# Loading MoE expert weights in 4 MB units and computing a block's gates and up-projections token-major

## The chip, the core and the metric

One NeuronCore of a Trainium2 chip runs the whole kernel. The metric is the device time of one execution in microseconds (us), lower is better. Engines: PE is TensorE (matmuls; PEld is its weight load), DVE is VectorE, ACT is ScalarE, POOL is GpSimd, and SP is the sequencer that issues most DMAs.

## The reference

One decoder layer on 256 tokens of width 1024, in float32. Cut to what matters here:

```python
proj = rmsnorm(x) @ w_in                      # 1024 x 5632
q_a, k_a, v_a, q_b, f_b, i_b, g_b, gate_a, gate_b = split(proj)
mixed = sigmoid(gate_a) * (y_a @ moba_up) + sigmoid(gate_b) * (y_b @ hgrn_up)
x = x + mixed @ w_out
h2 = rmsnorm(x);  top 4 of 32 experts for every token
gu = h2 @ w_gate_up[e] + b_gate_up[e]         # 1024 x 2048 = 8 MB for each expert
act = (clip(gu[1::2]) + 1) * swiglu(gu[0::2])
x = x + weight * (act @ w_down[e] + b_down[e])   # 1024 x 1024 = 4 MB for each expert
```

All 32 experts' weights are read, 12 MB each (the MB of this text are units of 1024 KB), 384 MB in all.

## The kernel before

**Front.** Projections run as split products: each weight piece is rounded to a high part on ACT (`round_hi`) and the rest is formed on DVE (`form_lo`, line 388), and PE adds high x high, low x high and high x low. `split_T` (line 1325) makes a 256-feature piece feature-major: the weights are the stationary side, 256 tokens move, 48 matmuls of 256 columns for a piece (24 where the depth is 512). `split` (line 1342) makes a unit token-major: 128 tokens are the stationary side and 512 weight columns move, 24 matmuls of 512 columns. The eight gate pieces ga0..3 and gb0..3, and the up-projections mu0..3 and hu0..3, use `split_T`; their mix is therefore feature-major as the output projection `mixed()` (line 1496) needs it. The list `PIECES` (line 47) sets the order and the buffer of every rounded piece, and `bank_units()` (line 66) the order of PE's units and who drains each.

**Expert weights.** There are 11 slots of 2 MB (16 KB in each partition): eight in S, then M's last four pages, EXTRA and B. A pair of experts takes 12 loads of 2 MB: 0 to 3 and 4 to 7 are gate/up weights, 8 to 11 the down weights. They go round the ring (`ring`, line 377), each by one DMA of 16 KB runs on SP's queue (`load`, line 403). SP issues a load once PE has used what was in its slot (`used`, line 447; `load_pair`, line 456). PE waits on a semaphore of each slot (`arrived`, line 1656). The last pair's last two loads go in parts of 8 KB and 4 KB runs, so that little is left when the last byte lands (line 475).

The pair-0 loads are issued early, between the loads of the front, as their space comes free (lines 408 to 445): 9 after the 10th weight group, 0 before the load of `mu`, 1 before `wo0`, 10 and 3 before `wo1`, 5 after hu3, 8 after the mix, 2 and 6 after the first half of the output projection and 4 and 7 after the second.

**Expert pair.** PE's loop `pair` (line 1753): `gate_up` (line 1664) for both experts of the pair, with weight columns in blocks of 512 as the moving side; `down` (line 1717); `gather` (line 1626), which reads the token rows X with a step of two elements (`hidden`, line 1586) as the stationary side; and `combine` (line 1648). The gate/up biases come in by four DMAs of 128 KB on ACT's queue (line 725), are rounded in one ACT copy (line 752) and one DVE subtract (line 1207), before ACT can do the router's exponentials (line 755).

Of the kernel before, what the change touches and what calls it, by code (L numbers as in the profile page):

```python
# [11 lines left out]
P = 128  # L12
T = 256
TT = T // P
D = 1024
# [26 lines left out]

GATES = [("g0", GB, 0), ("g1", GB, 1)] + [(f"ga{j}", GA0 + j // 2, j % 2) for j in range(4)] + \
# [10 lines left out]
    [("wo0", j, "dve", ("C", j), None) for j in range(2)] + \  # L54
    [("wo1", j, "dve", ("A", j), f"hu{2 * j + 1}") for j in range(2)]
# [10 lines left out]
def bank_units():  # L66
# [9 lines left out]
    for h in range(0, HEADS, 2):  # L76
# [5 lines left out]
    u += [(f"mu{j}", "dve") for j in range(4)] + [(f"hu{j}", "dve") for j in range(4)]  # L82
# [9 lines left out]
            "pos0": 5, "pos1": 2, "all": 7, "wT": 6}  # L92
UNITS = bank_units()
# [29 lines left out]
def hybrid_block(nc, A, out):  # L123
    ctx = ExitStack()
    with ctx:
# [7 lines left out]
        with ExitStack() as early:  # L133
# [3 lines left out]
            hT_hi = over("hT_hi", 2).rearrange("p (k t) -> p k t", k=KD)  # L137
            over("skip_b2", 1, F32)
            FRONT = early.enter_context(nc.sbuf_tensor("FRONT", [P, 512], F32))[:]
            MSK = early.enter_context(nc.sbuf_tensor("MSK", [P, 512], I32))[:, 0:NMASK * CHUNK]  # L140
            MSK = MSK.rearrange("p (m t) -> p m t", t=CHUNK)
# [9 lines left out]
            over("skip_s0", 8, F32)  # L151
# [3 lines left out]
            w_lo = [over(f"w_lo{s}", 4) for s in range(RING)]  # L155

        with ExitStack() as later:
            later.enter_context(nc.sbuf_tensor("skip_m0", [P, 1024 * 9], F32))  # L160
# [7 lines left out]
        B = sb("B", [P, 4096])  # L168
        XN = B[:, 0:TT * D].rearrange("p (t d) -> p t d", t=TT)
        M = sb("M", [P, 12 * 1024])  # L170


        S = sb("S", [P, 8, 4096])
# [14 lines left out]
        SF = S[:].rearrange("p s n -> p (s n)")  # L188
# [21 lines left out]
        def mpage(n, c=1):  # L210
            return M[:, 1024 * n:1024 * (n + c)]
# [5 lines left out]
        mixT = mpage(2, 2).rearrange("p (k t) -> p k t", k=KD)  # L217
# [4 lines left out]
        gaT, gbT = mpage(8, 2), mpage(10, 2)  # L222
# [5 lines left out]
        bias_raw = mpage(6)  # L228
        DN_B = mpage(6)[0:E, :]
        FW = mpage(6)  # L230
# [15 lines left out]
        EXTRA = sb("EXTRA", [P, 4096])  # L246
        slots = [S[:, s, :] for s in range(8)] + [mpage(8, 4), EXTRA[:], B[:]]

# [26 lines left out]
        def hi_part(where):  # L275

            buf, j = where
            if buf == "Q":
                return hi_a[:, 1024 * j:1024 * j + 1024].rearrange("p (k n) -> p k n", k=4)
            return {"A": hi_a, "B": hi_b, "C": hi_c}[buf][:, 2048 * j:2048 * j + 2048].rearrange("p (k n) -> p k n", k=KD)  # L280

# [12 lines left out]
        def bank(name):  # L294
            return PS[BANK_OF[AT_UNIT[name]]]


# [20 lines left out]
        osq_ready, rms_ready, sig_ready, yb_ready, mix_ready = (  # L318
            sem(n) for n in ("osq_ready", "rms_ready", "sig_ready", "yb_ready", "mix_ready"))
# [10 lines left out]
        mix_hi_ready, mix_lo_ready = sem("mix_hi_ready"), sem("mix_lo_ready")  # L330
# [4 lines left out]
        slot_loaded = [sem(f"slot_loaded{s}") for s in range(SLOTS)]  # L335
# [33 lines left out]
        wgu = A["w_gate_up"].rearrange("l e (s p k) n -> (l e) s p (k n)", p=P, k=2)  # L369
        wdn = A["w_down"].rearrange("l e (h p c) n -> (l e) h p (c n)", p=P, c=4)  # L370
        gu_slot = [w.rearrange("p (k n) -> p k n", k=2) for w in slots]
        dn_slot = [w.rearrange("p (k n) -> p k n", k=4) for w in slots]
# [4 lines left out]
        def ring(j, m):  # L377

            return (12 * j + m) % SLOTS, (12 * j + m) // SLOTS

        PER_ROUND = [(6 * E - 1 - n) // SLOTS + 1 for n in range(SLOTS)]

        def slot_src(e, m):

            src = wgu[e + m // 4, m % 4] if m < 8 else wdn[e + (m - 8) // 2, m % 2]
            return src[0] if len(src.shape) == 3 else src
# [12 lines left out]
        def _(sp):  # L399
# [3 lines left out]
            def load(e, j, m):  # L403

                slot = ring(j, m)[0]
                sp.dma_start(slots[slot], slot_src(e, m)).then_inc(slot_loaded[slot], 16)

            for n, what in enumerate(LOADS):
                if what == GB1:
                    load(0, 0, 9)  # L410
                if what == "mu":
                    filled(sp, "kT1")
                    load(0, 0, 0)
# [3 lines left out]
                if what == "wo1":  # L417
                    load(0, 0, 10)
# [37 lines left out]
            def load_pair(p, e, j, stop=12):  # L456
# [6 lines left out]
            for part, done in ((0, half_loaded), (1, slot_loaded[0])):  # L463
# [1404 lines left out]
```

## Time and profile before

| what | value |
|---|---|
| median of 3 runs | 1136.11 us (1135.65 to 1136.47) |
| the profiled execution, its own time | 1136.25 us |
| its span in the trace | 1134.5 us |
| PE busy | 1059.2 us (93%) |
| DVE / ACT / POOL busy | 348.4 / 222.7 / 38.9 us |
| moved by DMA | 439.17 MB (here 10^6 bytes), mean 387 GB/s |
| share of SP's queue in the 16 DMA engines' time | 92.6% |
| TensorE clock granted | full in all 40 slices |

The profile is one execution. "Busy" adds up an engine's instructions; the DMA share is the mean busy share of the 16 DMA engines, and packets of one engine overlap a little, so it can read 1.01. The front (everything ahead of the experts) ends near 221 us, the experts near 1124 us.

### The profile page before, as it was taken

How to read it: one execution, taken by the hardware profiler on the slowest of the kernel's cores; microseconds unless marked ns; L12 is line 12 of the kernel's file. 1: busy time of each engine (PE TensorE's matmuls, PEld its weight loads, DVE VectorE, ACT ScalarE, POOL GpSimd, SP SyncE). 2: the span in 40 equal slices, each digit the busy share in tenths (PEclk: the TensorE clock that was granted, in tenths of full speed). 3: DMA queues.
4: the chain of work that ended last, by engine and by line, in shares of the span. 5: the costliest groups of instructions: out<-in, count | busy, mean ns of one | idle time of the engine just before them, and what ended most of it. 6: DMA issues, size and time to landing. Idle time of an engine off the chain costs nothing.

```text
span 1134.5 us, 13360 instructions
## 1 busy us (share of the span) xinstructions
PE 1059.2 (93%) x5613; PEld 519.9 (46%) x5613; DVE 348.4 (31%) x686; ACT 222.7 (20%) x354; POOL 38.9 (3%) x32
## 2 busy tenths in 40 slices
PE   7999999999999999999988888888888898899896
PEld 7889999734343443434333333333333334233332
DVE  4984788422303222222222222222112020303022
ACT  6645674201010101011010010101010101010002
POOL 0390000000000000000000000000000000000000
PEclk9999999999999999999999999999999999999999
DMA  9545669999999999999999999999999999999994
GB/s 320 190 150 215 231 215 365 368 415 415 430 428 428 426 430 427 428 428 427 429 426 428 427 428 428 428 429 426 429 428 428 428 426 428 428 427 427 428 425 201
DMA packets 47489, 439.17 MB, mean 387 GB/s; under 512 B 5388, under 2 KB 7848, under 8 KB 22600
## 3 DMA queue, kind: packets, MB, share of 16 engines
q1 hardware_dynamic: 45136, 436.71, 92.6%
q10 hardware_dynamic: 2296, 1.61, 0.5%
q8 instruction: 47, 0.77, 0.3%
q14 instruction: 10, 0.08, 0.0%
HBM read 437.26 MB, written 1.05 MB: 386 GB/s over the span
## 4 chain that ended last, share of the span: by engine, by line
PE 57%; DMA 41%; DVE 1%; issue 0%; ACT 0%; another core or an unknown queue 0%; DVEq 0%
DMA S<-in_w_gate_up_dram 21%; PE PS L1671 20%; DMA S<-in_w_down_dram 12%; PE PS L1730 9%; PE PS L1338 9%; DMA B<-in_w_gate_up_dram 4%; PE PS L1652 4%; DMA EXTRA<-in_w_gate_up_dram 4%; PE PS L1632 3%; PE PS L1351 1%; PE PS L1354 1%; PE PS L1357 1%; PE PS L1712 1%; PE PS L1692 1%; PE PS L1318 1%; PE PS L1389 1%
## 5 line engine op out<-in xcount | busy, mean ns | idle before, releaser
L1671 PE MATMUL PS<-S,M 128*64 128x512 f32 x1520 | 340.0, 596 | 28.5 <-DMA S<-in_w_gate_up_dram 22.0
L1671 PEld LDWEIGHTS PS<-S,M 128*64 128x64 f32 x1520 | 105.3, 137 | 241.9 <-issue 195.7
L1171 DVE TENSOR_SCALAR M<-PS 128x256 f32<-128x256 f32 x64 | 27.0, 423 | 531.8 <-PE PS L1671 531.8
L1730 PE MATMUL PS<-S,M 128*64 128x512 f32 x736 | 164.7, 595 | 17.1 <-DMA S<-in_w_down_dram 17.1
L765 ACT ACTIVATE M<-M 128x256 f32<-128x256 f32 x64 | 26.7, 417 | 495.4 <-DVE M L1171 495.4
L1730 PEld LDWEIGHTS PS<-S,M 128*64 128x64 f32 x736 | 52.0, 137 | 119.8 <-issue 102.5
L770 ACT COPY M<-PS 64x512 f32<-64x512 f32 x31 | 17.9, 578 | 276.4 <-PE PS L1730 276.4
L1185 DVE COPY M<-PS 128x512 f32<-128x512 f32 x32 | 22.1, 692 | 127.7 <-PE PS L1712 127.7
L1632 PE MATMUL PS<-M,X 128*128 128x128 f32 x480 | 59.0, 281 | 0.0
L1632 PEld LDWEIGHTS PS<-M,X 128*128 128x128 f32 x480 | 57.7, 196 | 0.0
L1652 PE MATMUL PS<-M,SELT 128*128 128x512 f32 x120 | 55.5, 605 | 0.0
L392 DVE TENSOR_TENSOR w_lo<-S,hi_a 128x2048 fp32r<-128x2048 f32 (+1 forms) x24 | 46.5, 1954 | 20.0 <-ACT hi_a L569 20.0
L1671 PE MATMUL PS<-M 128*64 128x512 f32 x192 | 43.7, 597 | 3.4 <-DMA M<-in_w_gate_up_dram 2.4
L1671 PE MATMUL PS<-EXTRA,M 128*64 128x512 f32 x176 | 39.9, 595 | 3.6 <-DMA EXTRA<-in_w_gate_up_dram 3.6
L1179 DVE TENSOR_TENSOR M<-M 128x256 f32<-128x256 f32 x64 | 38.9, 607 | 2.2
L569 ACT CAST hi_a<-S 128x2048 fp32r<-128x2048 f32 (+1 forms) x24 | 38.4, 1622 | 5.7 <-PE PS L1338 3.2
L1671 PE MATMUL PS<-B,M 128*64 128x512 f32 x160 | 36.3, 596 | 3.4 <-DMA B<-in_w_gate_up_dram 3.4
L1652 PEld LDWEIGHTS PS<-M,SELT 128*128 128x128 f32 x120 | 21.6, 189 | 33.7 <-issue 33.7
L1162 DVE TENSOR_TENSOR M<-PS,SMALL 128x512 f32<-128x512 f32 x32 | 22.1, 692 | 34.1 <-PE PS L1632 32.8
L1338 PE MATMUL PS<-hT_lo,hi_a 128*128 128x256 f32 x224 | 31.6, 283 | 0.0
L1338 PE MATMUL PS<-hT_hi,w_lo 128*128 128x256 f32 x208 | 29.2, 283 | 0.0
L1338 PEld LDWEIGHTS PS<-hT_lo,hi_a 128*128 128x128 f32 x224 | 29.0, 192 | 0.0
(259 smaller groups left out, 978.3 us busy)
## 6 DMA issues: line engine op xcount, KB each, us to landing
S<-in_w_gate_up_dram SPq DMA_DIRECT2D x95, 2048.0 KB, 47.8
S<-in_w_down_dram SPq DMA_DIRECT2D x43, 2048.0 KB, 47.2
M<-in_w_gate_up_dram SPq DMA_DIRECT2D x12, 2048.0 KB, 46.5
EXTRA<-in_w_gate_up_dram SPq DMA_DIRECT2D x11, 2048.0 KB, 48.7
S<-in_w_in_dram SPq DMA_DIRECT2D x10, 2048.0 KB, 7.9
B<-in_w_gate_up_dram SPq DMA_DIRECT2D x10, 2048.0 KB, 48.5
B<-in_w_down_dram SPq DMA_DIRECT2D x7, 2048.0 KB, 48.2
EXTRA<-in_w_down_dram SPq DMA_DIRECT2D x6, 2048.0 KB, 48.0
```

The lines of the kernel that those rows point to most:

```text
L392: tensor_tensor(raw_part(what, j, lo=True), raw_part(what, j), hi_part(PIECES[n][3]), ALU.subtract).then_inc(lo_ready[PIECES[n][2]], 1)
L569: st.did(nc.scalar.copy(hi_part(PIECES[n][3]), raw_part(what, j)), hi_ready)
L765: nc.scalar.activation(sg[:, c], gate[:, c], ACT.Sigmoid, scale=ALPHA).then_inc(sigm_ready, 1)
L1162: v.tensor_tensor(hTe[:, 4 * part:4 * part + 4, :], src[:].rearrange("p (k s) -> p k s", k=4), n2w[:, 4 * part:4 * part + 4].unsqueeze(2). ...
L1171: v.tensor_scalar(gate[:, c], g2[:, :, 0], LIMIT, None, ALU.min).then_inc(gate_ready, 1)
L1179: v.tensor_tensor(act.rearrange("p (c q) -> p q c", c=4)[:, 64 * half:64 * half + 64, :], up[:, c].rearrange("p (q c) -> p q c", c=4), sg[ ...
L1185: v.tensor_copy(actT[b], (gu[1] if b else multi)[:].rearrange("p (c s) -> p c s", c=4)).then_inc(actT_ready, 1)
L1338: ins = mm(ps[:, T * a:T * a + T], w[:, k, P * a:P * a + P], x[:, k, :], start=(k == 0 and w is w_h and x is hi), stop=(k == kn - 1 and x ...
L1632: ins = mm(dst[:, P * a:P * a + P], hidden(tt, 4 * part + a), sel[:, tt, :], start=(tt == 0), stop=(tt == TT - 1))
L1652: mm(acc[tt][n][:], selT[:, P * tt:P * tt + P], Y[:, 512 * n:512 * n + 512], start=False, stop=True, skip_group_check=True)
L1671: ins = mm(gu[half][64 * g:64 * g + 64, :], hTe[:, k, tok], gu_slot[slot][:, kk, c:c + 512], start=(k == 0), stop=(k == KD - 1))
L1730: ins = mm(dst[64 * n:64 * n + 64, :], actT[b][:, k, 64 * kh:64 * kh + 64], dn_slot[slot][:, k, 512 * n:512 * n + 512], start=(kh == 0 and ...
```

## The change

1. A pair's loads are now joined two and two (0+1, 2+3, ... 10+11): one DMA of 4 MB with 32 KB runs into two neighbouring slots, issued when both slots are free. All slots lie in one tensor W so that neighbours adjoin. A unit stays two 2 MB loads (16 KB runs) where its slots are the last and the first of W, in pair 0, in the first four loads of pair 1, and from load 4 on in the last pair (`by_slots`).
2. So that a 4 MB unit is contiguous, a partition holds four rows of the gate/up matrix (before: two) and eight of the down matrix. The gathered rows of X are read with a step of four elements, and the moving weight columns of `gate_up` in blocks of 8 elements with a step of 16.
3. PE waits on semaphores of a pair's load number instead of the slot's.
4. Gates and up-projections are token-major (`split`), and the mixed output is turned by 16 transposes in four units mT0..3, the first three after hu1, hu2 and hu3, and the last inside `mixed()`. ACT rounds and DVE subtracts each turned chunk out of PSUM.
5. A second buffer hi_d, over slot 0, takes the high parts of GA1, GB1 and hu. So load 0 of pair 0 moves from before `mu` to after hu3. In the DVE's order both halves of GA1 come ahead of the softmax; a gate's first unit needs both halves of its group.
6. All biases come twice as wide: eight DMAs of 128 KB (four of them after the last `squares`), four ACT copies and four DVE subtracts of 64 partitions.

```diff
-    [(what, j, "dve", ("A", j % 2), "va1" if n < 2 else GATES[n - 2][0]) for n, (_, what, j) in enumerate(GATES)] + \
-    [("mu", j, "dve", ("Q", j), f"gb{2 + j // 2}") for j in range(4)] + \
-    [("hu", j, "dve", ("Q", j), f"mu{j}") for j in range(4)] + \
+    [(GB, j, "dve", ("A", j), "va1") for j in range(2)] + [(GA0, j, "dve", ("A", j), f"g{j}") for j in range(2)] + \
+    [(GA1, j, "dve", ("D", j), "kT1") for j in range(2)] + [(GB0, j, "dve", ("A", j), "ga1") for j in range(2)] + \
+    [(GB1, j, "dve", ("D", j), "ga3") for j in range(2)] + \
+    [("mu", j, "dve", ("QA", j), "gb1") for j in range(4)] + [("hu", j, "dve", ("QD", j), "gb3") for j in range(4)] + \
...
-        wgu = A["w_gate_up"].rearrange("l e (s p k) n -> (l e) s p (k n)", p=P, k=2)
-        wdn = A["w_down"].rearrange("l e (h p c) n -> (l e) h p (c n)", p=P, c=4)
+        wgu = A["w_gate_up"].rearrange("l e (u p k) n -> (l e) u p (k n)", p=P, k=4)
+        wdn = A["w_down"].rearrange("l e (p c) n -> (l e) p (c n)", p=P)
...
+        def by_slots(j, m, first_round):
+
+            return not first_round or ring(j, m) == 9 or j == 0 or j == 1 and m < 4 or j == PAIRS - 1 and m >= 4
...
+            def load_unit(e, j, m):
+
+                sp.dma_start(slots(ring(j, m), 2), unit_src(e, m)).then_inc(slot_loaded[m], 16)
...
                 if what == GB1:
-                    load(0, 0, 9)
-                if what == "mu":
-                    filled(sp, "kT1")
-                    load(0, 0, 0)
+                    load(0, 0, 8)
...
             filled(sp, "hu3")
+            load(0, 0, 0)
             load(0, 0, 5)
-            sp.wait_ge(mix_ready, 1)
-            load(0, 0, 8)
+            filled(sp, "mT3")
+            load(0, 0, 10)
...
-                for m in range(stop):
-                    used(p + (m - SLOTS) // 12, (m - SLOTS) % 12)
-                    load(e, j, m)
+                for m in range(0, stop, 2):
+                    if by_slots(j, m, first_round):
+                        for n in (m, m + 1):
+                            used(p + (n - SLOTS) // 12, (n - SLOTS) % 12)
+                            load(e, j, n)
+                    else:
+                        for n in (m, m + 1):
+                            used(p + (n - SLOTS) // 12, (n - SLOTS) % 12)
+                        load_unit(e, j, m)
...
             for j in range(4):
-                se.wait_ge(mix_step, j + 1)
-                st.did(nc.scalar.copy(mix_hi[:, 2 * j:2 * j + 2, :], mixT[:, 2 * j:2 * j + 2, :]), mix_hi_ready)
+                filled(se, f"mT{j}")
+                st.did(nc.scalar.copy(mixed_chunk(mix_hi, j), turned_mix(j)), mix_hi_ready)
...
+            def turn_mix(j):
+
+                ps = begin(f"mT{j}")
+                pe.wait_ge(mix_step, j + 1)
+                for a in range(4):
+                    c = unit_cols(j).start + P * a
+                    ins = tr(ps[:, P * a:P * a + P], ga[:, c:c + P], ident)
+                end(ins)
...
-                split_T(f"mu{j}", "mu", j, ya_hi, ya_lo, (ya_lo_ready, 2), kn=4)
+                up("mu", "mu", j, ya_hi, ya_lo, (ya_lo_ready, 2))
             pe.wait_ge(o_hi_ready, 1)
             for j in range(4):
-                split_T(f"hu{j}", "hu", j, o_hi, o_lo, (yb_ready, 1), kn=4)
+                up("hu", "hu", j, o_hi, o_lo, (yb_ready, 1))
+                if j:
+                    turn_mix(j - 1)
...
-                return X[:, tt, 256 * (k // 2) + k % 2:256 * (k // 2) + 256:2]
+                return X[:, tt, 512 * (k // 4) + k % 4:512 * (k // 4) + 512:4]
...
+                    cols = gu_slot[slot][:, kk, 1024 * half:1024 * half + 1024].rearrange("p (j g r) -> p j g r", g=2, r=8)
                     for g in range(2):
-                        c = 1024 * g + 512 * half
-                        ins = mm(gu[half][64 * g:64 * g + 64, :], hTe[:, k, tok], gu_slot[slot][:, kk, c:c + 512],
-                                 start=(k == 0), stop=(k == KD - 1))
+                        ins = mm(gate_rows(half, g), hTe[:, k, tok], cols[:, :, g, :], start=(k == 0), stop=(k == KD - 1))
```

## Rows read from the trace of the kernel before

**Rows 1.** Stretches: busy of PE, PEld, DVE, ACT, POOL; TensorE clock; DMA share; GB/s.

```profile
300.00:500.00 200.00, 200.00 (x955) 78.64 (x952) 43.84 (x111) 21.77 (x38) 0.00 (x0) 1.00 1.01 428
500.00:900.00 400.00, 361.32 (x1689) 138.82 (x1689) 77.74 (x192) 39.05 (x69) 0.00 (x0) 1.00 1.01 428
```

**Rows 2.** Chain that ended last, experts: start us, us, what.

```profile
276.32 10.30 PE PS L1671 x48
...
328.16 10.30 PE PS L1671 x48
...
726.37 3.65 PE PS L1671 x16
...
785.07 3.65 PE PS L1671 x16
...
1075.73 44.03 DMA S<-in_w_down_dram
```

**Rows 3.** Groups by line: count, busy us, mean ns, idle before with releasers.

```profile
L1671 PE MATMUL PS<-S,M 128*64 128x512 f32 x1520 | 340.0, 596 | 28.5 <-DMA S<-in_w_gate_up_dram 22.0 <-issue 4.6 <-DVE M L1173 1.8
...
L1632 PE MATMUL PS<-M,X 128*128 128x128 f32 x480 | 59.0, 281 | 0.0
```

**Rows 4.** Stretches of 2 KB, then 8 KB runs; columns as above.

```profile
181.00:186.00 5.00, 5.00 (x44) 5.00 (x43) 4.96 (x5) 0.62 (x1) 0.00 (x0) 1.00 1.04 387
1107.00:1113.00 6.00, 4.79 (x24) 1.95 (x26) 1.81 (x4) 0.20 (x1) 0.00 (x0) 1.00 1.01 419
```

**Rows 5.** DMA view: packets, MB, share; issues: count, size, median us to landing.

```profile
q1 hardware_dynamic: 45136, 436.71, 92.6%
...
S<-in_moba_up_dram SPq DMA_DIRECT2D x1, 2048.0 KB, 7.8
...
M<-in_b_gate_up_dram ACTq DMA_DIRECT2D x4, 128.0 KB, 10.6
```

**Rows 6.** SP's queue in order of time: start us, us until the last issue.

```profile
118.45 0.58 SPq L406 DMA_DIRECT2D S<-in_w_gate_up_dram  x1
...
186.99 0.33 SPq L406 DMA_DIRECT2D S<-in_w_gate_up_dram  x1
...
197.89 14.96 SPq L406 DMA_DIRECT2D S<-in_w_gate_up_dram  x4
222.74 2.04 SPq L468 DMA_DIRECT2D S<-in_w_down_dram  x2
227.89 29.36 SPq L406 DMA_DIRECT2D S<-in_w_gate_up_dram  x7
...
272.93 0.33 SPq L406 DMA_DIRECT2D B<-in_w_down_dram  x1
```

**Rows 7.** Line 406 between 240 and 245 us: the issue and its landing.

```profile
L406 SPq DMA_DIRECT2D S<-in_w_gate_up_dram x1: 328/328/328, 241.6 to 241.6; - x1
...
DMA to landing us min/median/max: 10.7/10.7/10.7
```

**Rows 8.** Chain, front: split (first two), a gate piece, then gb3 to hu3.

```profile
83.62 2.04 PE PS L1351 x8
85.65 1.81 PE PS L1354 x8
...
141.32 5.75 PE PS L1338 x48
...
157.96 28.99 PE PS L1338 x240
```

**Rows 9.** PE's groups by line, 100 to 222 us.

```profile
L1566 PE MATMUL PS<-CST,X 128*128 128x128 f32 x16 | 2.4, 274 | 0.1
```

**Rows 10.** DVE in order of time around the first scores.

```profile
113.84 2.29 DVE L392 TENSOR_TENSOR w_lo<-S,hi_a 128x2048 fp32r<-128x2048 f32 x1 [7.02 <-ACT hi_a L569]
118.91 0.56 DVE L995 TENSOR_TENSOR M<-PS,FRONT 128x384 f32<-128x384 f32 x1 [2.78 <-PE PS L1409]
```

**Rows 11.** ACT in order of time, same place.

```profile
113.71 1.07 ACT L560 COPY M<-PS 128x512 f32<-128x512 f32 x2
```

More of the change, by code:

```diff
@@ L150, in hybrid_block @@
             hi_b = over("hi_b", 4)
-            over("skip_s0", 8, F32)
+            hi_d = over("hi_d", 4)
+            over("skip_s1", 4, F32)
             hi_c = over("hi_c", 4)
@@ L242, in hybrid_block, with slots @@
         wT = mpage(7)[0:E, 512:768]
-        EXTRA = sb("EXTRA", [P, 4096])
-        slots = [S[:, s, :] for s in range(8)] + [mpage(8, 4), EXTRA[:], B[:]]
+        def slots(n, count=1):
+            at = (n + 1) % SLOTS
+            return W[:, 4096 * at:4096 * (at + count)]
         def h3(ap):
@@ L674, in _ @@
             gate_out(2)
-            round_hi(*GATES[4][1:])
             transposed_out("kT", kT)
+            for j in range(2):
+                round_hi(GA1, j)
             gate_out(3)
             for h in range(0, HEADS, 2):
-                round_hi(*GATES[5 + h // 2][1:])
+                round_hi(GB1 if h >= 4 else GB0, h // 2 % 2)
                 exps(h)
@@ L1009, in softmax_norm @@
                        prob_ready)
-            for n in range(2, 5):
-                lo(*GATES[n][1:])
+            for what in (GA0, GA1):
+                for j in range(2):
+                    lo(what, j)
             for h in range(0, HEADS, 2):
@@ L1338, in split_T, with split @@
                             ins = mm(ps[:, T * a:T * a + T], w[:, k, P * a:P * a + P], x[:, k, :],
-                                     start=(k == 0 and w is w_h and x is hi), stop=(k == kn - 1 and x is lo))
+                                     start=(k == 0 and w is w_h and x is hT_hi), stop=(k == KD - 1 and x is hT_lo))
                 end(ins)
-            def split(name, what, tt, hi=hT_hi, lo=hT_lo, lo_there=(hT_lo_ready, 1)):
+            def split(name, what, tt, hi=hT_hi, lo=hT_lo, lo_there=(hT_lo_ready, 1), kn=KD, half=0):
@@ L1348, in split @@
+                w_l = w_lo[s].rearrange("p (k n) -> p k n", k=kn)[:, :, 512 * half:512 * half + 512]
                 rows = slice(P * tt, P * tt + P)
-                pe.wait_ge(hi_ready, n + 1)
-                for k in range(KD):
-                    mm(ps[:].rearrange("p (j n) -> p j n", j=2), hi[:, k, rows], w_h[:, k], start=(k == 0), stop=False)
-                wait_lo(what, 1)
-                for k in range(KD):
-                    mm(ps[:], hi[:, k, rows], w_l[:, k, :], start=False, stop=False)
+                pe.wait_ge(hi_ready, last + 1)
@@ L1355, in split @@
+                for k in range(kn):
+                    mm(ps[:].rearrange("p (j n) -> p j n", j=2), hi[:, k, rows], w_h[:, k, 2 * half:2 * half + 2],
+                       start=(k == 0), stop=False)
+                wait_lo(what, 2 * half + 1)
+                for k in range(kn):
+                    mm(ps[:], hi[:, k, rows], w_l[:, k], start=False, stop=False)
                 pe.wait_ge(*lo_there)
-                for k in range(KD):
-                    ins = mm(ps[:].rearrange("p (j n) -> p j n", j=2), lo[:, k, rows], w_h[:, k], start=False,
-                             stop=(k == KD - 1))
+                for k in range(kn):
+                    ins = mm(ps[:].rearrange("p (j n) -> p j n", j=2), lo[:, k, rows], w_h[:, k, 2 * half:2 * half + 2],
+                             start=False, stop=(k == kn - 1))
@@ L1476, in _ @@
             probs_T(7)
-            split_T(*GATES[8])
+            split(*GATES[8])
             wait_drained(pe, "pT7")
```

253 lines of the change are left out of this document (141 added, 112 removed).

## The prediction

> **What bounds the kernel now.** I read the long stretches first: from 300 to 900 us the 16 DMA engines are busy all the time (share 1.01) and move 428 GB/s, and this doesn't change whether PE is busy for 200 of 200 us or for 361 of 400 [rows 1]. Then the chain of waits, which says who follows whom. Early on it runs through PE: pairs of experts start 328.16 - 276.32 = 51.8 us apart. Later it runs through DMAs that take 47 us to land, and the same point of a pair comes every 785.07 - 726.37 = 58.7 us [rows 2]. A pair is 24 MB, 25.17 million bytes, and at 428 GB/s that is 58.8 us. So PE needs 52 us for what the DMA engines bring in 59. It first lives on the loads made ahead and then waits, and its slack is 7 us for each pair. The last wait of all is for the last down weights: the chain's last DMA, 1075.73 + 44.03 = 1119.8 us [rows 2], with some 15 us of work behind it. The end is therefore set by three things: how many bytes are left when the DMA engines get busy for good, whether they idle after that, and their rate. What PE, ACT or DVE save or lose counts only where it moves one of the three.
>
> **The rate.** The trace has three run lengths with the engines full. In the stretch where half of w_out comes in (2 KB runs) they move 387 GB/s; in the last loads (8 KB runs) 419 [rows 4]; with 16 KB runs 428 [rows 1]. For one of 16 engines 2 KB then take 84.7 ns and 16 KB 612.5 ns. A line through both has 36.8 ns for each KB of 1000 bytes and 9.3 ns for a packet, whatever its size. It gives 422 GB/s for 8 KB, near the 419 of the row. A run of 32 KB replaces two packets by one and saves the 9.3 ns. A 4 MB unit has eight such runs on each engine: 74 ns less. Units: pairs 1 to 15 have 90 couples of loads; 2 of pair 1 and 4 of the last pair stay single, and 8 straddle the ends of W (ring place 9 on an even load: pairs 1, 3, 5, 7, 9, 10, 12, 14). That leaves 76, and 76 x 74 ns = **5.6 us gained**. Nothing in the trace is longer than 16 KB, so I bound it: 0 if longer runs are cut at 16 KB; and 8.0 us from the two nearest rows alone (8 KB 312.8 ns, so 13.1 ns for a packet). I take 5.6 because it lies on the longer base. The queue's 45136 packets [rows 5] should fall by 76 x 128 = 9700.
>
> **Idle at the start.** Space for load 0 of pair 0 is lost until hu3, since hi_d lies in slot 0. Today that load goes out at 118.45 us [rows 6], when the engines are half idle; now it goes out with load 5, at 186.99 in today's times. That is 2 MB, 4.9 us, more in the crowded stretch. But the stretch has holes. Loads 4 and 7 wait for the end of the output projection (the last of the four issues that begin at 197.89 ends at 212.85), the two half loads go at 222.74, and pair 1's first at 227.89 [rows 6]. A lone 2 MB load lands 7.8 us after its issue [rows 5] and moves for 4.9 us, so 2.9 us are latency. I went through the stretch load by load with these two numbers: before, about 6 us pass idle between load 5 and pair 1's load 9, of which 2 to 3 ahead of 227.89. The moved load fills most of that. The other four bias DMAs add 0.5 MB, 1.2 us.
> A new hole comes with the first 4 MB units. Loads 4 and 5 of pair 1 today go out one by one, in a row of seven issues 29.36 us long, 4.8 us apart [rows 6]. As a unit they wait for the second slot. The load ahead of them lands 10.7 us after its issue at 241.6, at 252.3 [rows 7]; the unit goes out at about 251.6 and its bytes flow from 254.5 on. That is a hole of 3 to 4 us. The next units lose nothing, as 4 MB are then under way, and what the row's gap before the load of 272.93 leaves idle today closes again. My replay ends with pair 1's last load landing 1.0 us later than before. From there the lead only grows (PE gives slots back faster than they fill). Bounds: +5 (hole and biases, nothing absorbed) and -1.
>
> **The front.** PE has no idle time there, so what it does counts. A gate piece takes 5.75 us, a token-major unit 2.04 + 1.81 + 1.81 = 5.66, or 5.46 without the first one's overlap [rows 8]: 8 x 0.2 = 1.6 to 2.3 us off. The eight up-projection units take (28.99 - 5.75)/8 = 2.9 us and will take 2.75: 1.2 off. On top come 16 transposes at 2.4/16 = 0.15 us [rows 9]: 2.4 added. One wait is new: ga2 needs both low parts of GA1, and ACT can round them only behind its two kT copies, from 114.8 on [rows 11]. With two roundings and, behind the first, two DVE subtracts of 2.29 [rows 10], the second low part is there near 121, by my reckoning 1 us after PE wants it. The softmax behind them moves from 118.91 [rows 10] to 121, which PE's order covers: it turns the first probabilities only after all of ga2 and two more scores. The mix steps end before PE comes back from the next up-projection. Net 0 to 1 us off; I take 0.2.
> The biases: four copies and four subtracts of 64 x 512 replace one of each. They must be there before the third step of the first gate/up, 10 us after 221. Landing 10.6 us [rows 5] after an issue near 212.85 (the output projection's end), plus some 4 us of work, is in time by 3 us.
>
> **PE in the pairs.** The moving weights are now read in 32-byte pieces and X with a step of four elements; the numbers of matmuls stay. I price both at nothing. A pair has 128 gate/up matmuls of 340.0/1520 = 0.224 us, 28.6 us, and 32 gather matmuls of 0.123 us, 3.9 us [rows 3]. What hides a slowdown is the 7 us of slack; the gather could take 2.5 times as long, the gate/up a quarter more.
> The Trainium skill, SBUF — State Buffer, section "Door 1: The DMA port swizzle", speaks against the step of four: SBUF has lines of 16 bytes, and a read that has only one hit in each line pays. By that page the gather's operand would slow, the 32-byte pieces would not. No run here shows it; it is a rival below.
>
> **Sum**, against the profiled execution's own 1136.25 us: -5.6 (rate) + 1.0 (start) - 0.2 (front) = 1131.45. The median of the runs lies 0.14 lower, so **1131.3 us**. About 0.2% (2.3 us) is what a measurement of this kernel can tell from no change.
>
> **Rivals.**
> *No gain in rate* (0.18). For: packets may be cut at 16 KB, or 428 GB/s may be the wall of something else than packets. Against: three run lengths lie on one line. Time: 1136.1 + 0.8 = 1136.9.
> *The gather slows* (0.10). A step of four elements doubles the weight reads. In the pairs 3.9 us more still fits into 7. But the first gather stands ahead of the first expert, with 32 matmuls, and puts off the slots that loads from 222.74 on wait for [rows 6]. The hole ahead of 227.89, which the moved load had filled, opens again by 2 to 4 us: 1131.3 + 3 = 1134.3. Against: a step of two shows no price today (0.123 us beside 0.15 for transposes).
> *The gate/up matmuls slow* (0.08): the other side. [...] It decides from 0.224 to 0.28 us for a matmul on, when 51.8 + 7 us reach the DMA's 58.8. At 0.336 (half as much again) a pair takes 66 us, and 16 pairs end near 221 + 16 x 66 + 10 = 1287; at 0.29 near 1150. Against: the high-part operand of `split`, read in two blocks, costs 2.04 us for eight where a plain one costs 1.81 [rows 8], and a part of that is overlap with what ran before.
> *The start loses more* (0.04): all of the 5 us, and the rate gains little: 1139 to 1141.
>
> **How the numbers follow.** The forecast has 0.60. Its own range is 1128.5 (8.0 from the rate, start -1) to 1134.5 (rate 5.6, start +4). To leave out no more than 2 in 10 the range goes up over the no-gain case to 1137.5, and the low end stays 1128.5. Faster by over 0.2% means under 1133.8: nearly all of the forecast and a third of the gather rival, 0.60. Slower means over 1138.4: the gate/up rival and the start, and a tail of no gain, 0.13. The rest, 0.27, is within.
>
> **What would show it.** Right: 431 GB/s in the long stretches at share 1.00; a pair every 58.4 us; about 35400 packets on SP's queue; a hole near 250; the first expert matmul within 1 us of 221; gate/up matmuls still 0.224 us. Wrong: 428 GB/s (no gain); gather matmuls over 0.15 us; PE with no idle time from 500 us on (the gate/up rival); an idle stretch of over 5 us after 230.

## The result, and the profile after

The changed kernel takes 1137.5 us (median of 16 runs, 1136.08 to 1139.74), the kernel before, in runs beside it, 1135.45 us (16 runs, 1134.45 to 1137.32). The ratio is 1.0021, 95% interval 1.0014 to 1.0028: slower by 2.1 us, where 1131.3 was forecast. The profiled execution of the changed kernel took 1138.16 us, its span is 1136.4 us.

The stretches, first the two long ones that answer to [rows 1], then some of the start (columns as there):

```profile
300.00:500.00 200.00, 200.00 (x893) 88.80 (x893) 42.04 (x102) 19.29 (x35) 0.00 (x0) 1.00 1.00 430
500.00:900.00 400.00, 395.56 (x1752) 171.03 (x1750) 81.01 (x203) 40.30 (x72) 0.00 (x0) 1.00 1.00 431
...
250.00:260.00 10.00, 10.00 (x39) 3.00 (x38) 2.00 (x6) 0.42 (x1) 0.00 (x0) 1.00 0.96 388
260.00:270.00 10.00, 10.00 (x47) 4.61 (x45) 2.33 (x6) 1.58 (x3) 0.00 (x0) 1.00 0.95 385
280.00:290.00 10.00, 10.00 (x50) 3.43 (x48) 0.00 (x0) 2.44 (x3) 0.00 (x0) 1.00 0.92 354
```

The rate came as forecast: 430 to 431 GB/s instead of 428, at a share of 1.00. But PE, which had idle time from 500 to 900 us before (361 of 400 us busy), is now busy for 396 of 400, and ahead of 300 us the DMA engines run below their rate three times.

The groups by line, PE's and then its weight loads, say why PE is full:

```profile
L1763 PE MATMUL PS<-W,M 128*64 128x512 f32 x2048 | 456.0, 597 | 5.8 <-issue 2.9 <-DVE M L1238 1.7 <-DMA W<-in_w_gate_up_dram 1.0
L1713 PE MATMUL PS<-M,X 128*128 128x128 f32 x480 | 114.4, 397 | 0.0
```

```profile
L1713 PEld LDWEIGHTS PS<-M,X 128*128 128x128 f32 x480 | 113.1, 329 | 0.0
```

The gather at L1713 (L1632 before) takes 114.4/480 = 0.238 us a matmul, where [rows 3] has 0.123: its weight loads alone keep PEld busy for 113.1 us. The gate/up matmuls, with their pieces of 32 bytes, still take 456.0/2048 = 0.223 us. The idle time behind the first row had been 28.5 us [rows 3, where the row covers 1520 of the 2048 matmuls] and is 5.8. PE's waits for weights say it whole: what waited for what, us in total, times, longest us. Before, the two largest of eight such rows, then the changed kernel's only two:

```profile
PE PS L1671 <- DMA S<-in_w_gate_up_dram: 22.0, 25, 2.0
...
PE PS L1730 <- DMA S<-in_w_down_dram: 17.1, 15, 1.3
```

```profile
PE PS L1821 <- DMA W<-in_w_down_dram: 5.9, 5, 1.9
...
PE PS L1763 <- DMA W<-in_w_gate_up_dram: 1.0, 3, 0.5
```

The eight rows of before add up to 53.4 us, which is all the slack that PE had in the run: 3.3 us for each of 16 pairs, and not the 7 of the forecast. The changed kernel has 6.9 us left. The slow gather takes 114.4 - 59.0 = 55.4 us more in pairs 1 to 15, and 3.7 more ahead of the first expert.

The chain that ended last shows the same in a pair (start us, us, what):

```profile
282.74 10.30 PE PS L1763 x48
...
323.78 7.46 PE PS L1713 x32
...
338.26 10.30 PE PS L1763 x48
...
1079.08 42.71 DMA W<-in_w_down_dram
1121.83 3.68 PE PS L1821 x16
```

Pairs start 338.26 - 282.74 = 55.5 us apart where [rows 2] had 51.8. The last landing that PE waits for is at 1079.08 + 42.71 = 1121.79 us, before at 1119.76: 2.0 us later, which is the loss. (This is what "the last landing" means from here on.)

The DMA view, SP's queue whole and then the loads by size (count, KB each, median us to landing):

```profile
q1 hardware_dynamic: 34192, 436.71, 92.0%
...
W<-in_w_gate_up_dram SPq DMA_DIRECT2D x51, 4096.0 KB, 35.6
W<-in_w_down_dram SPq DMA_DIRECT2D x25, 4096.0 KB, 32.4
```

There are 51 + 25 = 76 units, as counted, and 45136 - 34192 = 10944 = 76 x 144 packets fewer: 128 of data for each unit, as forecast, and 16 more that each DMA evidently brings with it, since a unit is one DMA where two were.

**The account of bytes.** If the engines are never short of work behind some point, the end is decided by what has been moved by then. I took GB/s times length stretch by stretch and added them up, in MB of 10^6 bytes:

```
moved by (us)      160     200     230     260     300
before            33.9    48.2    59.3    72.0    88.8
changed           32.3    47.1    58.1    70.3    86.0
```

At 300 us the changed kernel is 2.8 MB behind, 6.6 us at 430 GB/s. It also has 0.47 MB more to move in all (439.64 against 439.17), 1.1 us. If the rate gives the forecast's 5.6 us back, that makes 6.6 + 1.1 - 5.6 = +2.1 us, the 2.0 us of the last landing. And it does: from 300 us to that landing the kernel before moves 350.34 MB in 819.76 us (427.4 GB/s), the changed one 353.65 MB in 821.79 us (430.3 GB/s), which at 427.4 GB/s would have been 5.7 us more. So the gain of the forecast is there in full; what went wrong is 7.7 us of start and added bytes, where the forecast had 1.0. The runs had to say what makes up the 7.7.

### The profile page after: what moved, and what is told of

It reads as the page before. It is cut to its first block, busy times and chain, and to the rows that moved or that the text cites. A ratio compares the mean times of both kernels' runs of the same rounds, so it can differ in the third digit from the quotient of the medians.

```text
span 1136.4 us, 12828 instructions
## 1 busy us (share of the span) xinstructions
PE 1110.3 (98%) x5341; PEld 566.8 (50%) x5341; DVE 349.2 (31%) x691; ACT 224.3 (20%) x357; POOL 38.9 (3%) x32
## 2 busy tenths in 40 slices
DMA packets 36478, 439.64 MB, mean 387 GB/s; under 512 B 3980, under 2 KB 6440, under 8 KB 21320
## 3 DMA queue, kind: packets, MB, share of 16 engines
q1 hardware_dynamic: 34192, 436.71, 92.0%
## 4 chain that ended last, share of the span: by engine, by line
PE 83%; DMA 14%; DVE 1%; issue 0%; ACTq 0%; ACT 0%; DVEq 0%; SPq 0%
PE PS L1763 30%; PE PS L1821 18%; DMA W<-in_w_down_dram 14%; PE PS L1713 10%; PE PS L1733 4%; PE PS L1420 3%; PE PS L1424 3%; PE PS L1427 3%; PE PS L1406 3%; PE PS L1783 1%; PE PS L1803 1%; PE PS L1386 1%; PE PS L1673 1%; PE PS L1459 1%; DMA ROWS<-in_norm_w_dram 0%
## 5 line engine op out<-in xcount | busy, mean ns | idle before, releaser
L1763 PE MATMUL PS<-W,M 128*64 128x512 f32 x2048 | 456.0, 597 | 5.8 <-issue 2.9
L1763 PEld LDWEIGHTS PS<-W,M 128*64 128x64 f32 x2048 | 142.7, 137 | 288.8 <-issue 279.9
L1821 PE MATMUL PS<-W,M 128*64 128x512 f32 x1024 | 226.4, 594 | 5.9 <-DMA W<-in_w_down_dram 5.9
L1236 DVE TENSOR_SCALAR M<-PS 128x256 f32<-128x256 f32 x64 | 27.0, 423 | 494.9 <-PE PS L1763 494.9
L1821 PEld LDWEIGHTS PS<-W,M 128*64 128x64 f32 x1024 | 73.0, 137 | 145.2 <-issue 139.9
L1713 PE MATMUL PS<-M,X 128*128 128x128 f32 x480 | 114.4, 397 | 0.0
L1713 PEld LDWEIGHTS PS<-M,X 128*128 128x128 f32 x480 | 113.1, 329 | 0.0
L1733 PE MATMUL PS<-M,SELT 128*128 128x512 f32 x120 | 55.5, 605 | 0.0
L437 DVE TENSOR_TENSOR w_lo<-W,hi_a 128x2048 fp32r<-128x2048 f32 (+1 forms) x16 | 32.5, 2055 | 13.4 <-ACT hi_a L621 13.4
L1424 PE MATMUL PS<-w_lo,hT_hi 128*128 128x512 f32 x128 | 31.6, 389 | 0.0
L1240 DVE SCALAR_TENSOR_TENSOR M<-M 128x256 f32<-128x256 f32 x64 | 27.2, 425 | 2.2
L621 ACT CAST hi_a<-W 128x2048 fp32r<-128x2048 f32 (+1 forms) x16 | 26.6, 1695 | 1.6 <-DMA W<-in_w_in_dram 1.6
L1424 PEld LDWEIGHTS PS<-w_lo,hT_hi 128*128 128x128 f32 x128 | 24.0, 188 | 5.1
L1238 DVE TENSOR_SCALAR M<-PS 128x256 f32<-128x256 f32 x64 | 26.5, 414 | 0.0
## 6 DMA issues: line engine op xcount, KB each, us to landing
W<-in_w_out_dram SPq DMA_DIRECT2D x2, 2048.0 KB, 10.5
```

The costliest lines, as they stand in the source:

```text
L437: tensor_tensor(raw_part(what, j, lo=True), raw_part(what, j), hi_part(PIECES[n][3]), ALU.subtract).then_inc(lo_ready[PIECES[n][2]], 1)
L1240: v.scalar_tensor_tensor(out=up[:, c], in0=up[:, c], scalar=1.0, in1=gate[:, c], op0=ALU.add, op1=ALU.mult).then_inc(up_ready, 1)
L1424: mm(ps[:], hi[:, k, rows], w_l[:, k], start=False, stop=False)
L1713: ins = mm(dst[:, P * a:P * a + P], hidden(tt, 4 * part + a), sel[:, tt, :], start=(tt == 0), stop=(tt == TT - 1))
L1733: mm(acc[tt][n][:], selT[:, P * tt:P * tt + P], Y[:, 512 * n:512 * n + 512], start=False, stop=True, skip_group_check=True)
L1763: ins = mm(gate_rows(half, g), hTe[:, k, tok], cols[:, :, g, :], start=(k == 0), stop=(k == KD - 1))
```

## The experiments

Each ratio is against the kernel before, timed beside it: 1135.62 us for b_step4, a_step2, a_slots and a_early, 1135.56 for the a_perm kernels and a_ends, 1135.64 for b_late0 and the b_units and b_best kernels. Three theories stood against each other: the slow gather, which leads the first expert and gives the first slots back late; the 4 MB units at the first pairs; and the moved load 0.

### The gather's step alone, both ways

The changed kernel with a step of two, and the kernel before with a step of four (each then gathers features that don't fit its weights; the work is the same).

```diff
# a_step2: the changed kernel
-                return X[:, tt, 512 * (k // 4) + k % 4:512 * (k // 4) + 512:4]
+                return X[:, tt, 256 * (k // 2) + k % 2:256 * (k // 2) + 256:2]
# b_step4: the kernel before, the same two lines the other way round
```

> The kernel before with one edit: the gather reads X with a step of four, so it gathers the wrong features. Theory G: gather matmuls of 0.238 us, a first expert matmul 3.7 us later (224.5), and the time up by 2 to 4 us over the kernel before, as PE's slack of 7 us for each pair falls to 3. Theory H: the gather is hidden in the kernel before, within 1 us of it.

> The changed kernel with one edit: the gather reads X with a step of two elements again, so it gathers the wrong features (the number of instructions and of bytes is the same). Theory G (the step of four makes the gather's weight loads slower, 0.238 us for a matmul instead of 0.123, and this costs the time): the gather returns to about 0.123 us, the first expert matmul comes 3.7 us earlier, at 219.8, and the time falls from 1137.5 to 1131.3 to 1133.5. Theory H (the gather is hidden; the lost early load, the eight bias transfers and the waits for two slots at once cost the time): the gather gets faster all the same, but the time stays within 1.5 us of 1137.5.

Measured, b_step4: 1141.82 us, ratio 1.0054 (1.0041 to 1.0067), 6.2 us slower, where I expected 2 to 4. The gather takes 0.238 us a matmul there too, so the step of four is the whole cause of its price. Its start:

```profile
200.00:230.00 30.00, 29.80 (x156) 23.20 (x156) 11.60 (x41) 8.46 (x17) 0.00 (x0) 1.00 0.85 330
230.00:260.00 30.00, 28.25 (x125) 9.49 (x122) 7.43 (x23) 2.90 (x5) 0.00 (x0) 1.00 1.01 420
260.00:300.00 40.00, 40.00 (x176) 18.31 (x173) 8.00 (x21) 4.43 (x7) 0.00 (x0) 1.00 0.93 385
```

Before, these stretches have 370, 423 and 420 GB/s. The engines run dry (share 0.85) while PE gathers for the first pair, and again at 260 to 300 us while it gathers for the next. By 300 us the kernel is 88.8 - 85.9 = 2.9 MB behind: one line, a new step, loses at the start as much as the whole change does. Later on PE's slack did hide the gather (428 GB/s from 300 to 1000 us), but only just: of 53.4 us of waits for weights 9.6 are left. At the start there is no such slack, because the slots are full and each load waits for PE to free one.

Measured, a_step2: 1137.43 us, ratio 1.0018 (1.0008 to 1.0027). The gather is back at 0.123 us, and the time is the same: the gather's theory had 1131.3 to 1133.5 here, and by this run alone the gather would pass for hidden. Ten of its eleven runs scatter from 1135.03 to 1140.86 us, so differences of 1 us to it say little. Two waits stand in the gather's place, here among PE's waits (what waited for what: us in total, times, longest):

```profile
PE PS L1763 <- DMA W<-in_w_gate_up_dram: 28.7, 15, 4.6
...
PE PS L1783 <- DVE bias_parts L1276: 3.3, 1, 3.3
```

The 3.3 us are the biases. ACT in order of time (what follows the arrow ended its idle time):

```profile
212.24 1.74 ACTq L801 DMA_DIRECT2D M<-in_b_gate_up_dram  x4
228.30 2.29 ACT L807 CAST bias_parts<-M 64x512 fp32r<-64x512 f32 x4 [15.77 <-DMA M<-in_b_gate_up_dram]
```

The last of the four bias loads is there at 228.3, 16 us after the first one's issue at 212.24. The loads' own times in this execution, from issue to landing:

```profile
DMA to landing us min/median/max: 7.8/11.3/14.7
```

ACT needs all four, so the longest counts and not the median, which is all that [rows 5] shows. In the changed kernel the slow gather had hidden that. The other wait is for whole units: up to 4.6 us at a time, where PE in the kernel before waited 2.0 at most for a load of S. The total only says that PE has slack again; the length of one wait is what is new. The stretch 1080 to 1090 us, and PE in it and behind it, in order of time:

```profile
1080.00:1090.00 10.00, 7.97 (x30) 2.64 (x32) 0.36 (x2) 0.00 (x0) 0.00 (x0) 0.83 0.98 415
```

```profile
1082.03 5.03 PE L1763 MATMUL PS<-W,M 128*64 128x512 f32 x16 [3.54 <-DMA W<-in_w_gate_up_dram]
...
1114.24 10.52 PE L1821 MATMUL PS<-W,M 128*64 128x512 f32 x48
1125.90 3.70 PE L1907 MATMUL PS<-M,SELT 128*128 128x512 f32 x8 [1.14 <-DVE M L1297]
```

Behind an idle 3.54 us sixteen matmuls take 5.03 us instead of 3.58, and the granted clock of these 10 us is 0.83: a part of them ran at the lower level, 1.2 GHz. PE then comes to the last 48 down matmuls at 1114.2 and never waits for the last landing: the last bytes are there by 1121.0, some 2 us before the matmuls that use them. PE and no longer a DMA sets the end. So the gather was not the only cause; behind it stood others of the same size.

### The units

```diff
# a_slots: the changed kernel, no 4 MB unit at all
-            return not first_round or ring(j, m) == 9 or j == 0 or j == 1 and m < 4 or j == PAIRS - 1 and m >= 4
+            return True
# a_early: 2 MB slots through pair 2
+            return not first_round or ring(j, m) == 9 or j <= 2 or j == PAIRS - 1 and m >= 4
# a_ends: the same, and the whole last pair
+            return not first_round or ring(j, m) == 9 or j <= 2 or j == PAIRS - 1
```

> The changed kernel with every load by its own slot: no unit of 4 MB, all packets 16 KB, the layout of rows and the steps unchanged. It is what the units are worth by themselves. Theory G: the units gain 5.6 us in rate and lose 3 to 4 in holes at the start, so 1139 to 1140. Theory H: the units lose more than they gain, 1133 to 1136. The rate in the long stretches is 428 GB/s by both.

> The changed kernel with units only from pair 3 on (pairs 1 and 2 load slot by slot; 9 units fewer, 0.7 us of rate lost). If the holes between 250 and 300 us come from waiting for two slots, DMA moves over 420 GB/s from 250 to 300 (388 and 385 in two stretches of 10 us of the changed kernel) and the time falls by 2 to 3 us, to 1134.5 to 1135.5. If the holes come from PE giving back slots later (slow gather), the time stays within 1 us of 1137.5.

> The changed kernel (slow gather) with pairs 1, 2 and the whole last pair loaded slot by slot; beside a_early (1135.03) it differs by the last pair's two units alone. If PE's lag at the end is due to the last pair's units: 0.5 to 2 us below a_early, 1133 to 1134.5. If it is due to the slow gather alone: 1135.0 +- 0.4.

Measured: a_slots 1139.66 us (1.0039, 1.0026 to 1.0052), with 428 GB/s from 300 us on: all units together are worth 1139.66 - 1137.5 = 2.2 us in this kernel. a_early 1135.03 us (0.9995, 0.9986 to 1.0004): taking the units off pairs 1 and 2 gains 2.5 us, and the units that are left are worth 1139.66 - 1135.03 = 4.6 us. a_ends 1135.06 us, the same as a_early: with the slow gather the last pair makes no difference. The start of a_early:

```profile
230.00:260.00 30.00, 28.25 (x122) 9.35 (x118) 11.62 (x34) 4.45 (x10) 0.00 (x0) 1.00 1.01 421
260.00:300.00 40.00, 40.00 (x175) 18.59 (x174) 8.01 (x22) 4.76 (x8) 0.00 (x0) 1.00 0.95 396
```

From 230 to 260 us it moves 421 GB/s where the changed kernel moves 405: that hole belonged to the first units. The one from 260 to 300 us (396, before 420) stays: it is the slow gather's, as in b_step4, and with the fast gather it is gone (419 in a_step2, 424 in a_perm, both with their first units). In a_early PE waits 4.2 us in all for weights and runs its last 48 down matmuls without a break: with the slow gather PE itself is near its limit.

### A gather from contiguous columns

To make the gather cheap with the four-row layout, POOL copies X aside and back in turned order, before anything else needs it; the router's weights, the norm's weights and the last residual add follow that order, so the reference's output is computed.

```diff
# a_perm
...
+            for tt in range(TT):
+                for u in range(2):
+                    c = slice(512 * u, 512 * u + 512)
+                    ins = nc.gpsimd.tensor_copy(
+                        X[:, tt, c].rearrange("p (k q) -> p k q", k=4),
+                        aside[:, D * tt + 512 * u:D * tt + 512 * u + 512].rearrange("p (q k) -> p k q", k=4))
...
-                return X[:, tt, 512 * (k // 4) + k % 4:512 * (k // 4) + 512:4]
+                return X[:, tt, P * k:P * k + P]
# a_perm_bias: also the second four bias loads ahead of the last squares, not behind them
# a_perm_bias_ends: also by_slots of a_ends
```

> The changed kernel with X stored turned: POOL, idle until 44 us, rearranges each block of 512 columns of x once, so that the gather and the transposes read neighbouring elements; the router's weights are loaded in the same order, and the residual add and the four matmuls that add X at the end use strided views instead. Same result as the changed kernel's. By the look at a_step2 (gather fast, but PE waits 3.3 us for the biases, and at the end PE runs behind the last DMA): gather 0.123 us, 1136 to 1138, no gain, and PE waits over 2 us for bias_parts. Rival (the wrong rows of a_step2 made its odd behaviour): 1131 to 1133.5 and no wait for biases.

> a_perm with the second four bias DMAs issued ahead of the last squares, as soon as PE has read the high parts of the mix for the last time (some 4 us earlier). If the bias wait is what takes the fast gather's gain at the start, PE waits under 1 us for bias_parts and the time is 2 to 3 us below a_perm's. If the tail (PE behind the last DMA) sets the end, the start's gain does not show: within 1 us of a_perm.

> a_perm_bias with units only in pairs 3 to 14: pairs 1, 2 and the whole last pair load slot by slot (11 units fewer, 0.8 us of rate). With the holes at the start and the lag at the end gone it should be the fastest: 1130 to 1132, the last landing ahead of PE's last 16 matmuls by their own 3.7 us, as in the kernel before. If units only gain rate and neither hole nor lag cost anything, it is 0.8 us above a_perm_bias.

Measured: a_perm 1138.22 us (1.0018, 1.0009 to 1.0027), like a_step2 no gain by itself; PE waits 2.4 us for the biases here too, so that wait did not come from a_step2's wrong features. a_perm_bias 1135.97 us (0.9999, 0.9990 to 1.0008): once the gather is fast, the late biases cost 2.3 us. a_perm_bias_ends 1134.66 us (0.9992, 0.9983 to 1.0001), another 1.3, in intervals that overlap.

Those 1.3 us, if they are real, are not the first units': a_perm_bias already moves 428 GB/s from 230 to 260 us and 429 to 300, and both kernels have moved 88 MB by then (87.9 and 87.8). What differs is the end. From the chain of a_perm_bias (start us, us, what):

```profile
1114.63 10.47 PE PS L1842 x48
```

PE runs its last 48 down matmuls without waiting, and the last bytes are there by 1120.0, over 3 us before the matmuls that use them; a_perm_bias_ends waits for its last landing at 1118.41 and is done with the same matmuls at 1122.1 instead of 1125.1. PE had come late to them, as in a_step2: the granted clock from 1080 to 1120 us is 0.92, and 1.00 in the kernel before.

Still the sum missed the 1130 to 1132 that I expected, and against a_ends the fast gather brings only 0.4 us. The copies cost the front something: DVE in order of time at its first subtract, in a_perm_bias_ends,

```profile
14.11 3.31 DVE L936 TENSOR_TENSOR hT_lo<-W,hT_hi 128x2048 fp32r<-128x2048 f32 x1 [3.33 <-ACT hT_hi L646]
```

takes 3.31 us, with POOL's copies running until 15.3, and 2.29 in the kernel before; the first gather starts at 215.21 us, 0.9 later than in the changed kernel. And by 230 us this kernel had moved 58.0 MB, no more than the changed kernel (58.1; before 59.3): a deficit of that size is there without the slow gather and the first units.

### The moved load, and the front

```diff
# b_late0: the kernel before, only load 0 of pair 0 moved
                 if what == "mu":
                     filled(sp, "kT1")
-                    load(0, 0, 0)
...
             filled(sp, "hu3")
+            load(0, 0, 0)
             load(0, 0, 5)
```

> The kernel before with one step of the change alone: gate/up piece 0 of the first pair is issued after the eighth up-projection piece, ahead of piece 5, and no longer between the feature-major loads. No instruction of a compute engine is changed. The account of bytes puts the 1.2 MB that the changed kernel falls behind between 200 and 230 us down to this step: if that is right, the kernel comes out 1.5 to 3 us slower than before (1137 to 1138.5), with the deficit at 230 us near 1 MB. The prediction's step (the moved load fills the hole behind the waits of the last front pieces and the rest is absorbed) gives at most 1 us (to 1136.5).

> The feature-major front of before, with piece 0 issued early, and the expert part of the changed kernel whole: 4 MB units by 32 KB runs, gather of every fourth feature, eight bias loads. If the slow gather, the units at the first pairs and the moved load are what ate the gain, this one has only the moved load's 2.8 us back: 1134.5 to 1136, gather 0.238 us a matmul. If the token-major front costs something of its own beyond the moved load, it is below 1134; if the moved load is nothing, it stays at 1137 to 1138.5.

Measured, b_late0: 1137.52 us, ratio 1.0019 (1.0010 to 1.0028), 1.9 us slower; in its profiled execution (1137.13 us) the last landing is 0.9 us later than in the profile of before. The account of bytes: 2.1 MB behind at 160 us, 0.9 at 230, 0.4 at 300. Before, the engines run dry at 210 to 215 us (279 GB/s); the late load flows there (436 GB/s). So the forecast's mechanism, that it fills the hole, is right, and 1 to 2 us are what is left over, not the 2.8 of my account.

Then why doesn't the changed kernel catch up in the same hole? The DMA view from 210 to 225 us, b_late0 and then the changed kernel (queue, packets, MB, share of 16 engines):

```profile
DMA packets 439, 6.41 MB, mean 427 GB/s; under 512 B 48, under 2 KB 48, under 8 KB 48
...
q1 hardware_dynamic: 439, 6.41, 100.3%
```

```profile
DMA packets 505, 5.38 MB, mean 359 GB/s; under 512 B 92, under 2 KB 92, under 8 KB 205
...
q1 hardware_dynamic: 344, 4.92, 91.0%
q10 hardware_dynamic: 161, 0.46, 10.4%
```

The second set of bias loads runs there (q10). It takes 10.4% of the engines' 15 us, 1.6 us, for 0.46 MB, and beside it the queue of weights gets 4.92 MB through in 91.0%, 13.65 us, where 428 GB/s would need 11.5. The stretch moves 1.0 MB less than b_late0's, 2.4 us. It isn't the gather: a_step2, with the fast one, has the same (4.77 MB in 91.8%, and 10.5% for the biases). So the moved load and the wider biases want the same hole. No run leaves out the second set alone, so the 2.4 us are what goes with it, not its measured price.

Measured, b_units (before's front with load 0 early, and the change's expert part): 1139.95 us, ratio 1.0042 (1.0029 to 1.0056). That refutes what I expected: the early load is worth nothing here, and the kernel is slower than the changed one. At 230 us it is 0.5 MB ahead of it (58.6 against 58.1), at 300 us behind (85.8 against 86.0). With the slow gather, loads wait for slots and not for the engines (333 GB/s from 250 to 260 us, share 0.84): what counts is when PE starts the experts, 224.61 us here and 223.48 in the changed kernel. From there on it waits only 6.3 us for weights and runs its last 48 down matmuls without a break. The 1.1 us between the starts is about what the token-major front saves, and the profiled executions are 1.0 us apart (1139.16 and 1138.16); the medians are 2.4 us apart, and the rest of that stays unexplained.

### The version that the runs point to

The front of before with load 0 early; X turned by POOL from 82.8 to 94.9 us, behind its rotary work; the second bias loads before the last squares (they go out at 208.3, into the hole at 210); 2 MB slots for the first three pairs and the last; 4 MB units, 65 of them, for the rest. And the same without units.

```diff
# b_units_best against b_units
-            return not first_round or ring(j, m) == 9 or j == 0 or j == 1 and m < 4 or j == PAIRS - 1 and m >= 4
+            return not first_round or ring(j, m) == 9 or j <= 2 or j == PAIRS - 1
-                return X[:, tt, 512 * (k // 4) + k % 4:512 * (k // 4) + 512:4]
+                return X[:, tt, P * k:P * k + P]
...
# b_best_slots against b_units_best
-            return not first_round or ring(j, m) == 9 or j <= 2 or j == PAIRS - 1
+            return True
```

> The best version that the runs so far point to: the front of before with piece 0 early, X turned by GpSimd between 83 and 90 us so that the gather reads contiguous columns (0.123 us a matmul), the second four bias loads issued ahead of the last squares, 2 MB slots for the first three and the last pair, 4 MB units for pairs 3 to 14. If the losses add up as the account of bytes has them, 1131 to 1133, and 2.5 to 4.5 us faster than before. If TensorE's waits for whole units, and the lower granted clock behind them, take the gain at low slack, it stays at 1134 to 1136.

> The same as the version before this in the list, with 2 MB slots throughout: only the size of the run (16 KB instead of 32 KB) differs. By 48 units of two slots and 74 ns for each slot so loaded the units are worth 3.5 to 5 us, so this one is at 1135 to 1137. If the waits for whole units take back what the rate gives, the two are within 1 us.

Measured: b_units_best **1130.98 us** (1130.77 to 1131.14), ratio 0.9961 (0.9948 to 0.9974), 4.7 us faster than before and 6.5 faster than the changed kernel. b_best_slots 1136.28 us, ratio 1.0005 (0.9996 to 1.0014). The stretches of b_units_best, and the end of its chain:

```profile
200.00:230.00 30.00, 29.78 (x171) 20.29 (x171) 12.95 (x44) 9.69 (x20) 0.00 (x0) 1.00 1.00 376
230.00:260.00 30.00, 28.25 (x122) 9.38 (x120) 9.99 (x28) 3.32 (x6) 0.00 (x0) 1.00 1.01 428
260.00:300.00 40.00, 40.00 (x198) 16.31 (x196) 8.14 (x21) 4.81 (x8) 0.00 (x0) 1.00 1.01 428
300.00:1000.00 700.00, 659.64 (x3053) 257.56 (x3050) 143.31 (x358) 69.67 (x124) 0.00 (x0) 0.99 1.00 430
```

```profile
1070.26 44.18 DMA W<-in_w_down_dram
1114.48 3.68 PE PS L1810 x16
```

All holes behind 230 us are closed, 89.8 MB have moved by 300 us (before 88.8), and the last landing is at 1114.44, 5.3 us earlier than before. The units alone, between the two last kernels, are worth 1136.28 - 1130.98 = 5.3 us for 65 of them, 82 ns each, where the forecast had 74 ns (4.8 us); the intervals of the two ratios, 1 to 1.5 us each way, don't tell these apart. PE still waits up to 4.0 us for a unit here (22.0 us in 13 waits), and the clock of the whole execution is 0.989, yet PE's last matmuls still wait for the last landing.

## Why the prediction was wrong

By its own steps:

- **The bound**: right for this kernel, but closer to a second bound than it said. The account of bytes left at the start, idle stretches behind it, and the rate gives the measured +2.0 us of the last landing. PE is next: without its last 6.9 us of waits for weights the profiled execution would have taken 1138.16 - 6.9 = 1131.3 us, an estimate. With this gather PE alone allowed no more than the forecast.
- **The rate, -5.6 us**: right. 430 to 431 GB/s, 76 units, 128 data packets fewer for each. Isolated it came to 5.3 us for 65 units, where 4.8 were due. The rival without a gain is refuted.
- **The gather, priced at nothing**: this step failed. It said that 7 us of slack in each pair hide up to 2.5 times its time. They do, from 300 us on, but not at the first two pairs. There the slots are full, and PE's progress and not the engines' rate decides how much is loaded. And the slack was half of that: the 7 us are 58.8 - 51.8, true of a pair that has used up the loads made ahead, while over the whole run PE waited 53.4 us, 3.3 for each pair, and the slow gather takes 3.7 more. Done alone, the step of four costs 6.2 us. The rival had the mechanism right (weight reads doubled, slots put off ahead of 227.89) and its size wrong: it allowed 2 to 4 us at one place, and the holes are at two, 200 to 230 and 260 to 300 us. 2.9 MB are 6.8 us. The Trainium skill (SBUF — State Buffer, "Door 1: The DMA port swizzle") wants at least two hits in each line of 16 bytes, and the trace agrees: weight loads 196 ns with a step of two and 329 with four, 0.123 and 0.238 us a matmul, 0.223 us for the pieces of 32 bytes as before. It deserved more than a chance of 0.10.
- **Idle at the start, +1.0 us**: failed in its size. The load does fill the hole (b_late0) and alone leaves 0.9 to 1.9 us. The biases were put at their bytes, 1.2 us; the stretch in which they run lost 2.4. The hole of the first units, 3 to 4 us, was in the replay, which let the later gaps take most of it back; they did not: a_early gets 2.5 us back. All of it together with the gather is 7.7 us, above the bound of +5. These parts don't add up one by one: while slots are what is short, the other losses hide behind the gather, and each shows only when the one ahead of it is gone (a_step2, a_perm, a_perm_bias).
- **The front, -0.2 us**: right in sign, small in size. The first gather starts at 214.36 us instead of 215.22, 0.9 us earlier. The first expert matmul, by the slow gather, comes at 223.48 instead of 220.76, and not within 1 us.
- **The biases in time by 3 us**: wrong. Their median of 10.6 us to landing held, but all four have to be there, and the last took 13.5 us in the changed kernel (14.7 in a_step2) from an issue 1.3 us behind the first. Only the slow gather hid it.
- **Gate/up at nothing**: right, 0.223 us. Its rival is refuted. Its sums had the same fault as the slack: by its own 221 + 16 pairs + 10 PE reaches 1136 us at 56.6 us a pair, not at 58.8, and 0.29 us a matmul gives 1196, not 1150. The slow gather made the pair 55.5.

A thing that no step had: with a fast gather PE waits longer at a time for a unit than for a slot, and the granted clock falls behind such waits.

What stays open: of the 3.7 us between a_perm_bias_ends and b_units_best, which differ in the front, in where load 0 goes and in when X is turned, the runs don't give each its share. The 7.7 us of the changed kernel aren't split into shares either: each of its parts was measured, but in different company. Nor was b_units_best tried with units in pairs 1 and 2, or any kernel without the second set of bias loads.

## What to carry to other kernels

An engine's slack over the run is the sum of its waits, not the widest gap between two periods times the rounds: read it before you spend it. And slack in the steady state says nothing about the first rounds: where buffers are full at the start, time that the consumer loses ahead of the first freed buffers is missing at the end (6.2 us here for a step that adds 3.7 to each pair), so price each slowed step there separately. A hole in the DMA engines' time can be spent once; name everything that the change moves toward it. When a change has a gain that a count of packets supports and the whole shows none, take its parts off one at a time and then all together, since losses that hide behind each other each look free.

## What the runs showed of the hardware

- The stationary side read with a step of four float32 costs 329 ns for a weight load of 128 x 128, with a step of two 196, from contiguous columns 192; a matmul takes 0.238 and 0.123 us, and 0.117 (56.0/480) from contiguous columns.
- In b_units_best the last residual add reads X as the moving side with a step of 128 elements: 1051 ns for 512 columns, 592 before.
- Doubling the run from 16 to 32 KB raised the rate from 428 to 430 or 431 GB/s, 82 ns for a unit of 4 MB (b_units_best against b_best_slots), in line with a cost for each packet that doesn't grow with it. Each DMA has 16 packets beside its data (10944 = 76 x 144 fewer).
- Four loads of 128 KB on ACT's queue landed 7.0 to 13.5 us after their issues with SP's queue full, and 4.5 to 6.6 where it was running dry (b_units_best); with it full, their stretch moved 1.0 MB less than b_late0's, 2.4 us.
- Beside POOL's copies in SBUF a DVE subtract of 128 x 2048 took 3.31 us instead of 2.29 (a_perm_bias_ends), and two in a row 6.33 instead of 4.58 (b_units_best).
- Behind a PE idle for 3.5 us the granted clock of the next 10 us was 0.83, and sixteen matmuls took 5.03 us instead of 3.58.
